# Expert weights of a decoder block: neighbouring units loaded as pairs of 32 KB per partition

## What is computed

```python
logits = xt @ w_router + b_router
top_vals, top_idx = lax.top_k(logits, TOP_K)          # 4 of 32
gates = jax.nn.softmax(top_vals, axis=-1)
...
def expert_block(args):
    tok, e = args
    xb = x_pad[tok]
    gu = xb @ w1[e] + b1[e]                            # w1[e]: 1024 x 2048
    gate = jnp.minimum(gu[:, :F], SWIGLU_LIMIT)
    up = jnp.clip(gu[:, F:], -SWIGLU_LIMIT, SWIGLU_LIMIT)
    act = (up + 1.0) * gate * jax.nn.sigmoid(SWIGLU_ALPHA * gate)
    return act @ w2[e] + b2[e]                         # w2[e]: 1024 x 1024
```

## Time and profile before

| what | value |
|---|---|
| median of three runs | 1231.46 us (1230.99 to 1231.57) |
| profiled execution | 1230.75 us |
| its span, first to last instruction | 1228.7 us |
| TensorE busy | 1168.7 us, 95% |
| VectorE busy | 427.1 us, 35% |
| ScalarE busy | 206.2 us, 17% |
| moved by DMA | 462.31 MB, mean 376 GB/s |
| granted TensorE clock | 1.000 |

### The profile page before, as it was taken

The page is one execution under the profiler, slowest core; times in us unless marked ns, Lnnn a source line. Parts: engine busy times, 40 slices in busy tenths (PEclk is TensorE's granted clock), DMA queues, the critical chain, the costliest instruction groups (busy, mean ns, idle before and its releaser), DMA issues.

```text
span 1228.7 us, 17261 instructions
## 1 busy us (share of the span) xinstructions
PE 1168.7 (95%) x7138; PEld 584.6 (48%) x7138; DVE 427.1 (35%) x744; ACT 206.2 (17%) x303; POOL 58.6 (5%) x43
## 2 busy tenths in 40 slices
PE   9999999999999999999999999999999999899997
PEld 8888888888633333333333333333333333333332
DVE  5966765655722232222222222222222222222222
ACT  6444553534400000000000000000000000000001
POOL 0950000000300000000000000000000000000000
PEclk9999999999999999999999999999999999999999
DMA  9856437838999999999999999999999999999996
GB/s 312 267 207 224 152 137 269 310 140 350 409 428 427 429 428 428 428 429 428 429 428 428 429 428 428 428 428 429 429 428 428 429 428 429 428 429 429 428 425 281
DMA packets 57250, 462.31 MB, mean 376 GB/s; under 512 B 5761, under 2 KB 7490, under 8 KB 31906
## 3 DMA queue, kind: packets, MB, share of 16 engines
q1 hardware_dynamic: 53848, 458.97, 90.1%
q10 hardware_dynamic: 3370, 2.88, 0.8%
HBM read 459.71 MB, written 1.07 MB: 375 GB/s over the span
## 4 chain that ended last, share of the span: by engine, by line
PE 59%; DMA 37%; SPq 1%; ACT 1%; DVE 1%; issue 0%; DVEq 0%; ACTq 0%
DMA w_ring<-in_w 23%; PE ps L1241 15%; PE ps L1300 11%; DMA behind_watt<-in_w 7%; DMA behind_xb<-in_w 7%; PE ps L958 4%; PE ps L1390 3%; PE ps L966 3%; PE ps L964 3%; PE ps L965 3%; PE ps L1215 2%; PE ps L959 2%; SPq L578 1%; PE ps L978 1%; PE ps L1091 1%; PE ps L1093 1%
## 5 line engine op out<-in xcount | busy, mean ns | idle before, releaser
L1241 PE MATMUL ps<-w_ring,A_W 128*64 128x512 f32 x1232 | 278.1, 596 | 30.6 <-DMA w_ring<-in_w 29.1
L1830 DVE TENSOR_SCALAR A_W<-ps 128x512 f32<-128x512 f32 x32 | 22.1, 691 | 484.0 <-PE ps L1241 484.0
L1241 PEld LDWEIGHTS ps<-w_ring,A_W 128*64 128x64 f32 x1232 | 85.4, 137 | 205.8 <-issue 149.8
L1300 PE MATMUL ps<-w_ring,A_W 128*64 128x512 f32 x592 | 134.2, 595 | 0.0
L1472 DVE TENSOR_TENSOR w_parts<-w_ring,w_parts 128x1024 fp32r<-128x1024 f32 x76 | 110.0, 1466 | 57.2 <-ACT w_parts L690 56.3
L1241 PE MATMUL ps<-A_QK,A_W 128*64 128x512 f32 x416 | 94.2, 594 | 9.2 <-DMA A_QK<-in_w 8.7
L869 ACT ACTIVATE A_W<-ps 128x512 f32<-128x512 f32 x31 | 18.5, 597 | 438.3 <-PE ps L1281 438.3
L690 ACT ACTIVATE w_parts<-w_ring 128x1024 fp32r<-128x1024 f32 x75 | 78.9, 1058 | 64.7 <-PE ps L959 32.1
L865 ACT ACTIVATE A_W<-A_W 128x512 f32<-128x512 f32 x32 | 20.2, 630 | 394.8 <-DVE A_W L1830 394.8
L958 PE MATMUL ps<-hT_both,w_parts 128*128 128x512 f32 x224 | 79.3, 399 | 0.0
L1300 PEld LDWEIGHTS ps<-w_ring,A_W 128*64 128x64 f32 x592 | 40.4, 136 | 68.6 <-issue 66.9
(11 more groups left out here) (264 smaller groups left out, 1215.1 us busy)
## 6 DMA issues: line engine op xcount, KB each, us to landing
w_ring<-in_w SPq DMA_DIRECT2D x110, 2048.0 KB, 43.5
A_QK<-in_w SPq DMA_DIRECT2D x38, 2048.0 KB, 42.6
behind_watt<-in_w SPq DMA_DIRECT2D x19, 2048.0 KB, 43.5
w_ring<-in_w_in SPq DMA_DIRECT2D x36, 1024.0 KB, 7.4
behind_xb<-in_w SPq DMA_DIRECT2D x18, 2048.0 KB, 43.5
w_ring<-in_w SPq DMA_DIRECT2D x10, 1024.0 KB, 9.3
w_ring<-in_w_ret_branch SPq DMA_DIRECT2D x2, 2048.0 KB, 10.5
A_W<-in_w_out SPq DMA_DIRECT2D x1, 2560.0 KB, 13.2
```

The lines of the kernel that those rows point to most:

```text
L1241: mm = pe.matmul(o, XT[:, k, :], tile[:, j, c * HALF:(c + 1) * HALF], start=(k == 0), stop=(k == KC - 1))
L1300: mm = pe.matmul(ps[CAP * c:CAP * c + CAP, 3, :], lhs, w2_tile(flat)[:, q % W2_ROWS, c * HALF:(c + 1) * HALF], start=False, stop=(q == FQ ...
L1830: dve.tensor_scalar(gl, bank(0), LIMIT, None, ALU.min).then_inc(s.g, 1)
```

## The change

Units n and n + 1 of an even n become neighbours. `PAIR_ROWS` = 4 rows of w1, or all eight of w2 that a partition holds, lie together in HBM, 32 KB, and the order of rows follows from that (`w1_both`, `w2_both`, `by_unit_row`, `in_unit_rows`, the loads of router and gain). The ring is reordered so that places 0 and 1, 2 and 3, 4 and 5, 8 and 9 are neighbours in memory; places 6 and 7 are not. From unit 28 on (`FIRST_PAIR`), units in such places are loaded as two transfers, one for partitions 0 to 63 and one for 64 to 127, each with 32 KB a partition, both after one wait for the second place. Both raise the pair's semaphore, and TensorE waits for both before either unit. Units in places 6 and 7, the first units and the last four are loaded one by one as before, their runs in HBM 16 KB out of each 32 KB. The columns of the first products are read in another order, so that hidden column 8p + j comes out where the rows of w2 need it: block c takes runs of four columns with gaps of four (`hidden_columns`). In the early loads unit 1 goes before unit 0, and unit 9 and unit 7 change turns. The diff, cut to its core:

```diff
+PAIR_ROWS = 2 * W1_ROWS
...
-        ring = [w1_part(1), w1_part(0), w2_part(0), w2_part(1), A_QK[:, UNIT_WORDS:2 * UNIT_WORDS], behind_watt[:, :],
-                A_QK[:, 0:UNIT_WORDS], w1_part(3), w1_part(2), behind_xb[:, :]]
+        ring = [w1_part(0), w1_part(1), w2_part(0), w2_part(1), two_behind_qk[:, 0:UNIT_WORDS],
+                two_behind_qk[:, UNIT_WORDS:2 * UNIT_WORDS], A_QK[:, 0:UNIT_WORDS], behind_xb[:, :], w1_part(2), w1_part(3)]
+        ring_pair = {0: w1_flat[:, 0:2 * UNIT_WORDS], 2: w2_flat[:, 0:2 * UNIT_WORDS], 4: two_behind_qk[:, :],
+                     8: w1_flat[:, 2 * UNIT_WORDS:4 * UNIT_WORDS]}
+        FIRST_PAIR = 26
+
+        def hidden_columns(row, c):
+            return row.rearrange("p (g q c j) -> p g c q j", g=2, c=2, j=W2_ROWS)[:, c // 2, c % 2]
...
+        def w1_both(e, u):
+            rows = PAIR_ROWS * P
+            return w1[bass.ds(e, 1), u // 2 * rows:(u // 2 + 1) * rows, :].rearrange("e (p j) n -> p (e j) n", j=PAIR_ROWS)
...
+        def w2_both(e):
+            return w2[bass.ds(e, 1), :, :].rearrange("e (p j) n -> p (e j) n", j=FQ)
...
         def place(n):
-            in_halves = n >= RING and n % RING < HALF_UNITS
-            return ring[n % RING], s_unit[n % RING], 16 * (n // RING + 1 + in_halves)
+            at = n % RING
+            if at == RING - 3:
+                return ring[at], s_odd, 16 * (n // RING + 1), 1
+            if at == RING - 4:
+                return ring[at], s_pair[at // 2], 16 * (n // RING + 1), 1
+            halves = (2, 1, 0, 0, 0)[at // 2] if n >= RING else 0
+            return ring[at], s_pair[at // 2], 32 * (n // RING + 1) + 16 * halves, 2
...
+        def load_expert_w1(sp, e, i, used):
+            for u in range(0, W1_UNITS, 2):
+                n = w1_number(i, u)
+                if n >= FIRST_PAIR and n % RING in ring_pair:
+                    to, source = ring_pair[n % RING].rearrange("p (j n) -> p j n", j=PAIR_ROWS), w1_both(e, u)
+                    sp.wait_ge(s_used, used + n + 1 - RING + 1)
+                    for rows in (slice(0, P // 2), slice(P // 2, P)):
+                        sp.dma_start(to[rows], source[rows]).then_inc(s_pair[n % RING // 2], 16)
+                    continue
+                for one in range(2):
+                    if n + one >= RING + HALF_UNITS:
+                        sp.wait_ge(s_used, used + n + one - RING + 1)
+                        load_w1(sp, e, u + one, n + one)
...
         def by_unit_row(view):
-            return view.rearrange("q (u p j) -> q u j p", p=P, j=W1_ROWS)
+            return view.rearrange("q (u p j) -> q u j p", p=P, j=PAIR_ROWS)
...
+            load_w1(sp, 0, 1, 1)
+            sp.wait_ge(s_wl, LAST_UNIT)
             load_w1(sp, 0, 0, 0)
-            sp.wait_ge(s_wl, LAST_UNIT)
-            load_w1(sp, 0, 1, 1)
...
             sp.wait_ge(s_wu, LAST_BRANCH + UNITS)
-            load_w1(sp, 1, 3, 7)
+            load_w2(sp, 0, 1, 9)
             sp.wait_ge(s_wo, 3)
             load_w2(sp, 0, 0, 8)
             sp.wait_ge(s_x2, 2 * TT)
-            load_w2(sp, 0, 1, 9)
+            load_w1(sp, 1, 3, 7)
...
-                        mm = pe.matmul(o, XT[:, k, :], tile[:, j, c * HALF:(c + 1) * HALF],
+                        mm = pe.matmul(o, XT[:, k, :], hidden_columns(tile[:, j, :], c),
                                        start=(k == 0), stop=(k == KC - 1))
...
-                    pe.matmul(o, sel1[0:BIAS_ROWS, :], bias[:, c * HALF:(c + 1) * HALF], start=False, stop=False)
+                    pe.matmul(o, sel1[0:BIAS_ROWS, :], hidden_columns(bias[:, 0:2 * F], c), start=False, stop=False)
```

More of the change, by code:

```diff
@@ L546, in _ @@
             for i in range(1, TURN):
-                for u in range(HALF_UNITS if i == 1 else 0, W1_UNITS):
-                    n = w1_number(i + 1, u)
-                    sp.wait_ge(s_used, n - RING + 1)
-                    load_w1(sp, i + 1, u, n)
-                for u in range(W2_UNITS):
-                    n = w2_number(i, u)
-                    sp.wait_ge(s_used, n - RING + 1)
-                    load_w2(sp, i, u, n)
+                load_expert_w1(sp, i + 1, i + 1, 0)
+                load_expert_w2(sp, i, i, 0)
@@ L570, in _ @@
                 sp.wait_ge(s_used, w2_number(e, u) - RING + 1)
-                flat, landed, _ = place(w2_number(e, u))
+                flat = ring[w2_number(e, u) % RING]
                 for h in range(2):
                     rows = slice(h * W2_ROWS // 2, (h + 1) * W2_ROWS // 2)
-                    sp.dma_start(w2_tile(flat)[:, rows, :], w2_source(e, u)[:, rows, :]).then_inc(s_w2half[n] if h else landed, 16)
+                    sp.dma_start(w2_tile(flat)[:, rows, :], w2_source(e, u)[:, rows, :]).then_inc(s_w2half[2 * n + h], 16)
@@ L575, in _ @@
             sp.wait_ge(s_used, N_UNITS - 1 - RING + 1)
             for j in range(W2_ROWS):
-                flat, _, _ = place(N_UNITS - 1)
+                flat = ring[(N_UNITS - 1) % RING]
                 sp.dma_start(w2_tile(flat)[:, j, :], w2_source(N_EXP - 1, 1)[:, j, :]).then_inc(s_quarter[j], 16)
@@ L1259, in hidden @@
                 for u in range(W1_UNITS):
-                    flat, landed, count = place(first + u)
-                    pe.wait_ge(landed, rounds + count)
+                    flat, landed, count, loads = place(first + u)
+                    pe.wait_ge(landed, loads * rounds + count)
                     if u == 1 and row_done is not None:
@@ L1323, in hidden_last @@
                 for u in range(W1_UNITS):
-                    flat, landed, count = place(w1_number(N_EXP - 1, u))
+                    flat, landed, count, _ = place(w1_number(N_EXP - 1, u))
                     pe.wait_ge(landed, count)
@@ L1336, in down_halves @@
             def down_halves(n, e, u, row):
-                flat, landed, count = place(w2_number(e, u))
+                flat = ring[w2_number(e, u) % RING]
                 for h in range(2):
@@ L1341, in down_halves @@
                         scatter_tile(1, sc_w, y_sb).then_inc(s_scattered, 1)
-                    pe.wait_ge(*((s_w2half[n], 16) if h else (landed, count)))
+                    pe.wait_ge(s_w2half[2 * n + h], 16)
                     for j in range(h * W2_ROWS // 2, (h + 1) * W2_ROWS // 2):
@@ L1372, in down_last @@
                 down_halves(2, i, 0, last_row)
-                flat, _, _ = place(w2_number(i, 1))
+                flat = ring[w2_number(i, 1) % RING]
                 for j in range(W2_ROWS):
```

57 lines of the change are left out of this document (29 added, 28 removed).

## The result

The changed kernel takes 1980.76 us (median of 7 runs, 1939.98 to 2023.97) against 1231.3 us (median of 7 runs of before): 749 us slower, 1.609 times the time. The forecast of 1232.4 us and the whole range to 1258 us are wrong. What happened is the rival "the halves collide" (given 0.15, 1899 us). The executions of this kernel lie further apart than those of before, and the profiled one is the longest (2023.97 us, span 2021.8 us).

What follows compares the result with a forecast made beforehand. Expert weight transfers at 428 GB/s were taken to set the pace, TensorE having a little slack. Median 1231.46 less 2.4 us (packets) plus 3.3 us (tail) gave 1232.4 us; forecast's own range 1229 to 1235, wider range 1224.5 to 1258 us.

Steps and rivals of the forecast that it cites:

- the halves collide: Rival: paired 64-partition transfers reach only part of SBUF's write paths, 208 GB/s, 1899 us; lasting 0.15, dissolving 0.05 (1257 to 1307).
- 1899, 1704 and 1840 us: Collision totals for paired units at 208 GB/s (bias loads), 245 GB/s (decay table) and 218 GB/s (Trainium skill).
- the 3.3 us of the tail: Last expert: TensorE starts unit 184 only when 185 lands, so its last weight matmuls end 3.3 us later.
- Part 1, packets: Paired expert weight loads: 32 KB packets save 4.6 ns for each packet saved, 2.4 us in all (2.1 to 5.3).
- Part 2, waits before a pair: SyncE's wait for the second place delays the first unit 3.4 to 4.9 us; deep queue hides it, cost nothing.
- Part 3: TensorE gets both units together: steady pace stays that of the transfers, but the end comes 3.3 us later.
- Part 4, runs of four: First products' column reads in runs of four words: taken as 0; slack covers a loss up to 17%.
- Part 5, the rest: Slower L1691 additions near 308 us hidden by TensorE's backlog, early load order and router loads: all 0.
- The rate rises: Rival: longer runs keep the transfers at their best rate, 433 GB/s; 1228.3 us, or 1225.0 without the tail; chance 0.27.
- Cut up again: Rival: the queue cuts 32 KB into smaller packets, so only the tail counts; 1234.8 us; chance 0.08.
- Runs of four: Rival: TensorE pays for the column reads in first products above 17% loss; 1590 us at twice the time; chance 0.03.

Runs made afterwards that it cites:

- even_odd: The changed kernel with each pair's two 64-partition transfers taking even and odd partitions instead of lower and upper ones; 1231.51 us.
- middle_first: The changed kernel with each pair as three transfers, partitions 32 to 95, then 0 to 31, then 96 to 127; 1958.32 us.
- one_transfer: The changed kernel with each pair as one transfer over all 128 partitions, 32 KB on each; 1231.22 us, ratio 0.9997.
- by_columns: The changed kernel with each pair as two transfers over 128 partitions, 16 KB on each, all pairing waits kept; 1235.88 us, ratio 1.0034.
- tail_apart: one_transfer with the last expert's first two units loaded apart, each with a semaphore of its own; 1229.73 us, ratio 0.9987.
- no_pairs: The changed kernel with no unit loaded as a pair, the new order of rows and columns kept; 1236.01 us, ratio 1.0034.
- offset_4: The changed kernel with four 256 KB copies inside HBM before the first pair, in pieces lying apart; the three such kernels took between 1936 and 2184 us.
- offsets_apart: The changed kernel with nine copies inside HBM before the first pair, meant to set neighbouring engines two packets apart; 2135.1 us.

## Why the prediction was wrong, step by step

**The step that failed** is the choice between rival and forecast, not a term of the sum. The collision was seen, with its row (208 GB/s while bias loads into 32 partitions run) and its price; 1899 us is within 5% of 1980.76. It got 0.15 because of two arguments. The first, that 29.5 to 31.5 us with a load on all partitions is no better at 245 GB/s, compared two stretches with different packets: 58 of the first's 181 are of 8 KB or more, and carry at least 0.475 of its 0.73 MB; none of the second's are. The row for large packets into few neighbouring partitions was the one that the prediction itself called the nearest, and it should have carried the forecast. The second, that engines 45 us deep in their queues fall out of step and use both halves, had no row behind it. In the change they do drift apart in part: the 256 packets of two unpaired units, 9.8 us of work at the full rate, start within 23 us of each other near 775 us and within 58 us near 1065 us (the 16 KB packets in the trace's records). The rate did not come back. Twelve kernels, the change among them, now load neighbouring partitions in parts, one with the halves on two queues and seven with copies meant to set engines apart, and their means between 700 and 1100 us lie between 194 and 241 GB/s: in none did the collision dissolve. The Trainium skill (SBUF — State Buffer, Door 1) had the result: 64 partitions from 0 reach half of the ports, 218 GB/s at best; 205 to 218 GB/s here agree. The section of that page on two DMAs to both halves has the rest, that the two serialize. By the port table of Door 1 every second partition reaches all ports, and even_odd agrees. By its port table a range from 32 to 95 reaches all ports as well; middle_first doesn't bear that out as I priced it, 1958 us in place of 1559, and the measurement decides.

The price was 4% low. (1899, 1704 and 1840 us each hold the 3.3 us of the tail, which their working doesn't show; 1231 + 128 x 4.7 alone is 1833.) It left the unpaired units at full rate, while the slices in which they go reach 370 GB/s at best, some only 252 to 318, and a few slices of the pairs lie below 205. How the 82 us divide was not measured.

**Part 1, packets: right in kind, mis-sized.** one_transfer against by_columns: 1235.88 - 1231.22 = 4.7 us, against the 2.4 forecast and within 2.1 to 5.3. Over 64 x 8 packets that is 9.1 ns for each one saved. one_transfer also has one transfer where by_columns has two, but even_odd, with two transfers and 32 KB packets, is as fast (1231.51 us), so it is the packets. The line through 2 KB and 16 KB gave 4.6; the stretch set aside for its first-use delays gave 10.4.

**Part 2, waits before a pair: right.** The rate of one_transfer has no gap where the pairs begin (395 to 500 us, slices of 2.6 us, none under 387 GB/s) nor between 700 and 1100 us (none under 413), 431 GB/s on average in both.

**Part 3, steady pace right, tail right.** TensorE's timeline of the end, one_transfer, then tail_apart, against the earlier trace rows:

```profile
1166.29 7.09 PE L1268 MATMUL ps<-w_ring,A_W 128*64 128x512 f32 x32 [1.34 <-DMA w_ring<-in_w]
...
1185.82 3.65 PE L1268 MATMUL ps<-two_behind_qk,A_W 128*64 128x512 f32 x16 [1.11 <-DMA two_behind_qk<-in_w]
...
1219.98 2.85 PE L1417 MATMUL ps<-A_W 64*128 64x512 f32 x12
```

```profile
1165.92 7.09 PE L1273 MATMUL ps<-w_ring,A_W 128*64 128x512 f32 x32 [1.34 <-DMA w_ring<-in_w]
...
1218.29 2.85 PE L1422 MATMUL ps<-A_W 64*128 64x512 f32 x12
```

Unit 184 starts 1.11 us late, when its pair has landed, and nothing waits after it: from its start to the last matmuls are 34.16 us (34.8 forecast). In no_pairs the same two lines stand at 1191.91 and 1226.08, 34.17 us: it loads each unit alone but still counts both units of a neighbouring pair on one semaphore, so it has the tail without the saving. In tail_apart the wait is gone, but the end moves by 1.7 us and not by 3.3. TensorE now runs without a wait for weights from 1165.92 us on. There it starts units 180 and 181, which landed together, and has both still to do (7.09 us), where before had only 181 left; that is what makes it late. The expectation for tail_apart left this out.

**Part 4, runs of four: right.** The 16 matmul instructions of a unit take 3.65 us in one_transfer as in before.

**Part 5, the rest: wrong by 2 us, in two places.** The claim was that the additions of L1691 are hidden and that the transfers run without a gap from 283 us. SyncE's timeline and the DMA view of 300 to 350 us (slices of 1.25 us), one_transfer; after them the same DMA row and issue of before:

```profile
312.12 0.33 SPq L442 DMA_DIRECT2D behind_xb<-in_w  x1
323.89 0.33 SPq L585 DMA_DIRECT2D w_ring<-in_w  x1
```

```profile
GB/s 433 419 413 433 459 419 459 406 419 419 433 419 433 419 419 419 419 419 39 79 242 400 380 328 347 400 406 419 426 426 426 446 465 406 419 433 419 433 419 446
```

```profile
321.81 0.33 SPq L543 DMA_DIRECT2D w_ring<-in_w  x1
```

```profile
GB/s 419 439 433 433 446 446 446 433 419 433 419 419 419 419 419 433 419 419 229 360 393 347 419 380 413 426 419 439 433 419 478 426 393 433 446 419 446 419 433 433
```

Near 323 us the queue was dry in before already (a slice of 229), since the next loads wait for TensorE to have used the units. The additions now take 1076 ns each in place of 679, 1.6 us more for the four. TensorE and with it the next issue come 2.1 us later (323.89 against 321.81), and the gap deepens to 39 and 79 GB/s. From 300 to 350 us 19.83 MB move in place of 20.90, which is 2.5 us at 428 GB/s. TensorE caught up with its own backlog, as predicted; the transfers, which set the end, did not. So the sum for a version at full rate should have read 1231.46 - 4.7 + 3.3 + 2.1 = 1232.2 us; one_transfer measured 1231.22, and 0.6 us of the difference is the work behind unit 184 (34.16 in place of 34.80 us). No run took the longer additions away, so that they cost these 2 us is read from the two timelines and not tested.

This also accounts for no_pairs, which has the tail and the gap but no saving: 1231.46 + 3.3 + 2.1 = 1236.9 us, measured 1236.01. Its profiled execution is its longest (1237.28 us), and in it the issue comes at 325.42, 3.6 us later than in before.

**The other rivals.** "The rate rises": not in the change; in one_transfer 431 against 428 GB/s, which the packets' saving explains. "Cut up again": no, the paired loads stand as 32 KB packets in the records, and one_transfer has 7178 packets where by_columns has 11764. "Runs of four": no, by part 4.

## What to carry over

Give each transfer all 128 partitions, or ones spread over them as in even_odd; don't cut a tile into lower and upper partitions, from one queue or two. When the nearest row of a trace shows a slow stretch with the very property that a change adds, let it carry the forecast until a row (not an argument) speaks against it. Where transfers set the end, look for the moments at which their queue is dry, and for the work behind the last load: there microseconds of compute engines count.

## What was unexpected of the hardware

- Two transfers of 64 partitions move 205 to 218 GB/s when the partitions lie together and 431 GB/s when each takes every second one, same bytes, same 32 KB packets.
- The half rate doesn't need all engines. In the records of offset_4 the packets of the pair take near 2.55 us while those of the copies inside HBM, in flight at the same time, still take 1.21 us, and in offsets_apart, from 418.28 us on, two packets at a time are enough for 2.56 us. Two of 32 KB in 2.56 us are 25.6 GB/s together, no more than the 27.0 GB/s of a single one at 1.213 us. Why is open; which engine carries a packet isn't recorded.
- Several kernels with copies meant to push engines apart were slower than the change itself (2179.67 and 2135.1, one run each, against 1980.76 us), with slices down to 131 GB/s. That wasn't followed up.
- An addition of 128 x 512 words takes 679 ns with a step of two words and 1076 ns with a step of four, on the read or on the written side.
